# The projection products of two embedding stages, issued in four lots inside the feed-forward stage ahead of each

## The reference, cut to what matters

```python
    for layer in range(DEPTH):
        j = layer // 2
        hn = rmsnorm(h, g_mix[layer])
        if layer % 2 == 0:
            mix = even_mixer(hn, ...)
        else:
            mix = odd_mixer(hn, positions, ...)
        h = h + mix
        h = h + swiglu(rmsnorm(h, g_ffn[layer]), w_gate[layer], w_up[layer], w_down[layer])
        gate = jax.nn.sigmoid(rmsnorm(h, g_ple[layer]) @ w_ple_gate[layer])
        h = h + gate * (p[layer] @ w_ple_proj[layer])
```

## Time and profile before

| | |
|---|---|
| median of 3 runs | 1310.94 us |
| lowest and highest | 1304.89 and 1313.02 us |
| span of the profiled execution | 1305.6 us |
| device time of the profiled execution | not given by the page |
| TensorE busy | 1226.4 us, 94% |
| VectorE, ScalarE busy | 727.1 and 462.5 us |

### The profile page before, as it was taken

One profiled execution on the slowest core, in us unless ns is written; L12 is line 12 of the kernel. 1 busy time (PEld: TensorE's weight loads), 2 busy tenths in 40 slices (PEclk: granted clock), 3 DMA queues, 4 the chain that ended last, 5 costly groups with the idle time before them and its releaser, 6 DMA issues.

```text
span 1305.6 us, 16407 instructions
## 1 busy us (share of the span) xinstructions
PE 1226.4 (94%) x6372; PEld 839.8 (64%) x6372; DVE 727.1 (56%) x1358; ACT 462.5 (35%) x741; POOL 28.8 (2%) x61
## 2 busy tenths in 40 slices
PE   6998999999898989999988997899999999999995
PEld 5997888876676768888866965544444444454442
DVE  5787877785657768777868997511221222221212
ACT  5444444444555654444454425211111111111112
POOL 0000000000000000000000300000000000000000
PEclk9999999999998999999999998899999999999999
DMA  8467777753430196666533464989999999999994
GB/s 286 158 224 268 255 258 257 257 194 117 166 129 1 65 364 249 247 246 245 200 138 129 146 200 149 407 324 413 421 430 430 428 428 428 429 429 429 428 429 168
DMA packets 120060, 358.09 MB, mean 274 GB/s; under 512 B 8666, under 2 KB 67731, under 8 KB 104626
## 3 DMA queue, kind: packets, MB, share of 16 engines
q1 hardware_dynamic: 113408, 331.85, 65.5%
q0 software_dynamic: 6336, 25.17, 4.9%
q10 hardware_dynamic: 242, 0.06, 0.0%
HBM read 352.58 MB, written 1.05 MB: 271 GB/s over the span
## 4 chain that ended last, share of the span: by engine, by line
PE 80%; DVE 12%; ACT 3%; DMA 2%; issue 1%; ACTq 0%; SPq 0%; DVEq 0%
PE ps L2702 16%; PE ps L419 14%; PE ps L420 14%; PE ps L421 14%; PE ps L2733 8%; PE ps L2691 4%; DVE xn L2302 3%; DMA second_expert<-in_moe_w_up 2%; DVE w_lo L393 2%; PE ps L2747 1%; PE ps L1023 1%; PE ps L2748 1%; PE ps L894 1%; PE ps L1635 1%; PE ps L829 1%
## 5 line engine op out<-in xcount | busy, mean ns | idle before, releaser
L393 DVE TENSOR_TENSOR w_lo<-dense_weights,w_hi 128x1024 fp32r<-128x1024 f32 (+1 forms) x228 | 273.1, 1211 | 100.9 <-ACT w_hi L388 100.2
L388 ACT CAST w_hi<-dense_weights 128x1024 fp32r<-128x1024 f32 (+1 forms) x228 | 234.9, 1042 | 257.7 <-PE ps L421 225.6
L419 PE MATMUL ps<-w_hi,xT_lo 128*128 128x512 f32 (+1 forms) x608 | 244.9, 403 | 19.1 <-DVE xT_lo L2349 5.2
L420 PE MATMUL ps<-w_lo,xT_hi 128*128 128x512 f32 (+1 forms) x608 | 238.4, 392 | 0.0
L421 PE MATMUL ps<-w_hi,xT_hi 128*128 128x512 f32 (+1 forms) x608 | 237.9, 391 | 0.0
L419 PEld LDWEIGHTS ps<-w_hi,xT_lo 128*128 128x128 f32 x608 | 116.2, 191 | 48.0 <-issue 14.9
L421 PEld LDWEIGHTS ps<-w_hi,xT_hi 128*128 128x128 f32 x608 | 116.2, 191 | 24.6
L420 PEld LDWEIGHTS ps<-w_lo,xT_hi 128*128 128x128 f32 x608 | 116.4, 191 | 23.3 <-issue 0.7
L2840 DVE TENSOR_TENSOR hnT<-ps,g_bc 128x512 f32<-128x512 f32 x32 | 22.1, 692 | 157.3 <-PE ps L2733 157.3
L2849 DVE SCALAR_TENSOR_TENSOR cmask<-g_v,ps 128x256 f32<-128x256 f32 x32 | 13.5, 421 | 166.5 <-ACT g_v L2791 166.5
L2791 ACT ACTIVATE g_v<-ps 128x256 f32<-128x256 f32 x32 | 12.3, 384 | 206.0 <-PE ps L2702 206.0
(11 more groups left out here) (407 smaller groups left out, 1725.1 us busy)
## 6 DMA issues: line engine op xcount, KB each, us to landing
ada_w<-in_ada_w POOLq DMA_DIRECT2D x12, 2048.0 KB, 11.7
dense_weights<-in_w_gate SPq DMA_DIRECT2D x22, 1024.0 KB, 7.2
dense_weights<-in_w_up SPq DMA_DIRECT2D x22, 1024.0 KB, 9.4
dense_weights<-in_w_down SPq DMA_DIRECT2D x22, 1024.0 KB, 5.0
dense_weights<-in_moe_w_gate SPq DMA_DIRECT2D x11, 2048.0 KB, 19.0
dense_weights<-in_moe_w_up SPq DMA_DIRECT2D x11, 2048.0 KB, 23.4
second_expert<-in_moe_w_gate SPq DMA_DIRECT2D x11, 2048.0 KB, 18.4
second_expert<-in_moe_w_up SPq DMA_DIRECT2D x11, 2048.0 KB, 22.9
```

What stands on the lines that cost most here:

```text
L388: act.copy(split_view(w_hi, name, i, j), piece(name, i, j)).then_inc(hi_ready, 1)
L393: dve.tensor_tensor(split_view(w_lo, name, i, j), piece(name, i, j), split_view(w_hi, name, i, j).bitcast(F32), ALU.subtract).then_inc(pie ...
L419: pe.matmul(out, left[1], right[0], start=start, stop=False)
L420: pe.matmul(out, left[0], right[1], start=False, stop=False)
```

## The change

Both projections get a place of their own in g_bc and are loaded by one transfer each: the first behind the loads of ev_in, the second behind those of od_out, once the query products have been made. The eight matmuls of a layer are cut into four lots of two, (i, t) for column half i and token tile t, each with a bank 2i + t that keeps it until VectorE reads it in the embedding stage:

- (1,1), bank 3: behind the gate and up product of the first feed-forward block;
- (0,0), bank 0: behind the transposes of the last hidden block, ahead of its down product;
- (0,1), bank 1: behind the last down product;
- (1,0), bank 2: one matmul behind the norm's second bank of transposes, one behind the fourth.

The norm's transposes ahead of the embedding go to banks 4, 6, 5, 7 in place of 0 to 3, and the gate products to banks 4, 6 and 5, 7. In layer 1 `pe_sums` moves to the middle of the first gate product, VectorE's `dve_cols` ahead of the first additions to h, and TensorE waits for these columns before the second gate product. The final gain's semaphore is shared with the projections' transfers.

```diff
-ITEMS = [... ("ple0", 2, 1, 1), ... ("ple1", 2, 1, 1), ...]
+ITEMS = [... ("ple0", 2, 1, 0), ... ("ple1", 2, 1, 0), ...]
...
+        ple_proj = g_bc
...
@@ ups
                 load_b("od_up", 1, q_up_rows[2], q[:, 2])
+                sp.wait_ge(ple_used, 1)
                 for k in range(2):
                     sp.dma_start(q_up_rows[k], q[:, k]).then_inc(small_landed, 16)
...
+            def projection(layer):
+                if layer == 1:
+                    sp.wait_ge(odd_up.lat_turned, 2)
+                sp.dma_start(ple_proj[:], a["w_ple_proj"][layer].rearrange("(k p) n -> p k n", p=P)).then_inc(ple_landed, 16)
...
             columns("ev_in", a["ev_w_in"][0], [2048, 1536, 512, 1024, 0])
+            projection(0)
...
             columns("od_out", a["od_w_out"][0], [0, 512])
+            projection(1)
             ffn(1)
...
@@ NormStage
-                return ps[:, c // 2 + (4 if self.index == 0 else 0), (c % 2) * S:(c % 2 + 1) * S]
+                banks = {0: (4, 5, 6, 7), 2: (4, 6, 5, 7), 5: (4, 6, 5, 7)}.get(self.index, (0, 1, 2, 3))
+                return ps[:, banks[c // 2], (c % 2) * S:(c % 2 + 1) * S]
...
                     last.then_inc(self.turned, 1)
+                    if between is not None and b in between:
+                        between[b]()
...
@@ FfnStage.pe
                     if n >= 1:
                         down(n - 1, it)
+                    else:
+                        projection.up(pe, 1, 1)
+
+                projection = ple[self.layer]
                 self.run(pe, step)
                 turn(last_block, None)
+                projection.up(pe, 0, 0)
                 down(last_block, None)
+                projection.up(pe, 0, 1)
...
@@ PleStage
+            GATE_BANKS = ((4, 6), (5, 7))
+
+            def up(self, pe, i, t, ks=range(2)):
+                if (i, t) == (1, 1):
+                    pe.wait_ge(ple_landed, 16 * (self.layer + 1))
+                for k in ks:
+                    last = pe.matmul(ps[:, 2 * i + t, :], pT[:, self.layer, k, t * P:(t + 1) * P],
+                                     ple_proj[:, k, i * 512:(i + 1) * 512], start=(k == 0), stop=(k == 1))
+                if (i, t, k) == (1, 0, 1):
+                    last.then_inc(ple_used, 1)
...
-                tokens_by_columns(pe, self.name, 0, (0, 1), rest=lambda: self.norm.wait_rest(pe))
-                up(0)
+                def rest():
+                    self.norm.wait_rest(pe)
+                    if self.between is not None:
+                        self.between.pe_sums(pe)
+
+                tokens_by_columns(pe, self.name, 0, self.GATE_BANKS[0], rest=rest)
                 if self.between is not None:
-                    self.between.pe_sums(pe)
-                tokens_by_columns(pe, self.name, 1, (4, 5), rest=lambda: up(1))
+                    pe.wait_ge(self.between.cols, 1)
+                tokens_by_columns(pe, self.name, 1, self.GATE_BANKS[1])
                 if self.following is not None:
-                    stay_busy(pe, 3, 6)
+                    stay_busy(pe, 4, 6)
...
@@ PleStage.dve
                     if i == 1 and self.between is not None:
-                        self.between.dve_cols(dve, own)
                         split_upto(dve, split_lo, self.name, i, 2)
                         conformer.spread_weights(dve, own, 0, 4)
                     split_upto(dve, split_lo, self.name, i, 3)
-                    dve.wait_ge(ple_used, 2 * self.layer + i + 1)
+                    if i == 0 and self.between is not None:
+                        self.between.dve_cols(dve, own)
+                    dve.wait_ge(ple_used, self.layer + 1)
...
-            norms[2].pe(pe)
+            norms[2].pe(pe, between={1: lambda: ple[0].up(pe, 1, 0, (0,)), 3: lambda: ple[0].up(pe, 1, 0, (1,))})
...
-            norms[5].pe(pe)
+            norms[5].pe(pe, between={1: lambda: ple[1].up(pe, 1, 0, (0,)), 3: lambda: ple[1].up(pe, 1, 0, (1,))})
```

More of the change, by code:

```diff
@@ L57 @@
 SLOTS = 2
-ITEMS = [("ev_in", 5, 1, 0), ("ev_out", 2, 2, 0), ("ffn0", FF_BLOCKS, 2, 1), ("ple0", 2, 1, 1), ("od_in", 5, 2, 0),
-         ("od_up", 2, 0, 1), ("od_out", 2, 1, 0), ("ffn1", FF_BLOCKS, 2, 1), ("ple1", 2, 1, 1), ("conv_in", 4, 2, 0),
+ITEMS = [("ev_in", 5, 1, 0), ("ev_out", 2, 2, 0), ("ffn0", FF_BLOCKS, 2, 1), ("ple0", 2, 1, 0), ("od_in", 5, 2, 0),
+         ("od_up", 2, 0, 1), ("od_out", 2, 1, 0), ("ffn1", FF_BLOCKS, 2, 1), ("ple1", 2, 1, 0), ("conv_in", 4, 2, 0),
          ("conv_out", 2, 1, 0)]
@@ L326, in build @@
         pieces_used = sem("pieces_used")
-        ple_used = sem("ple_proj_used")
+        ple_landed, ple_used = sem("ple_proj_then_gain_landed"), sem("ple_proj_used")
         up_used = sem("od_up_used")
@@ L522, in load_b @@
                     sp.wait_ge(up_used, 4)
-                elif stage is not None and stage.startswith("ple"):
-                    sp.wait_ge(ple_used, 2 * int(stage[-1]) + k + 1)
                 elif stage is not None:
@@ L568, in ple @@
                 w = a["w_ple_gate"][layer].rearrange("(k p) n -> p k n", p=P)
-                q = a["w_ple_proj"][layer].rearrange("(k p) n -> p k n", p=P)
                 for i in range(2):
                     load_a(name, i, [cols8(part_a(name, i))], [w[:, :, i * 512:(i + 1) * 512]])
-                    load_b(name, i, part_b(name, i)[:, 0:2 * 512].rearrange("p (k n) -> p k n", k=2),
-                           q[:, :, i * 512:(i + 1) * 512])
+            def projection(layer):
+                if layer == 1:
+                    sp.wait_ge(odd_up.lat_turned, 2)
+                sp.dma_start(ple_proj[:], a["w_ple_proj"][layer].rearrange("(k p) n -> p k n", p=P)).then_inc(ple_landed, 16)
             columns("ev_in", a["ev_w_in"][0], [2048, 1536, 512, 1024, 0])
+            projection(0)
             w = a["ev_w_out"][0].rearrange("(k p) n -> p k n", p=P)
@@ L816, in factors, with pe @@
                 dve.tensor_tensor(rstd[:, 2], rstd[:, 0], rstd[:, 1], ALU.mult).then_inc(self.made, 1)
-            def pe(self, pe, gains=None):
+            def pe(self, pe, gains=None, between=None):
                 if gains is not None:
@@ L1013, in __init__ @@
                 self.layer, self.name, self.norm, self.between, self.following = layer, f"ple{layer}", norm, between, following
-            def pe(self, pe):
[L1016 to L1025, removed]
-                tokens_by_columns(pe, self.name, 0, (0, 1), rest=lambda: self.norm.wait_rest(pe))
-                up(0)
+            GATE_BANKS = ((4, 6), (5, 7))
[7 more added lines that the diff above has]
+                    last.then_inc(ple_used, 1)
+            def pe(self, pe):
+                def rest():
[3 more added lines that the diff above has]
+                tokens_by_columns(pe, self.name, 0, self.GATE_BANKS[0], rest=rest)
                 if self.between is not None:
-                    self.between.pe_sums(pe)
-                tokens_by_columns(pe, self.name, 1, (4, 5), rest=lambda: up(1))
+                    pe.wait_ge(self.between.cols, 1)
+                tokens_by_columns(pe, self.name, 1, self.GATE_BANKS[1])
                 if self.following is not None:
-                    stay_busy(pe, 3, 6)
+                    stay_busy(pe, 4, 6)
             def act(self, act):
@@ L1045, in act @@
                             act.wait_ge(self.used, 2 * (2 * self.layer + i - 1) + t + 1)
-                        act.activation(ple_th[:, t], ps[:, 4 * i + t, :], ACT.Tanh,
+                        act.activation(ple_th[:, t], ps[:, self.GATE_BANKS[i][t], :], ACT.Tanh,
                                        scale=rstd[:, 1, t:t + 1]).then_inc(self.tanh, 1)
@@ L1061, in dve @@
                         dve.wait_ge(self.tanh, n)
-                        dve.scalar_tensor_tensor(out=ple_a[:, t], in0=ple_th[:, t], scalar=1.0, in1=ps[:, 4 * i + 2 + t, :],
+                        dve.scalar_tensor_tensor(out=ple_a[:, t], in0=ple_th[:, t], scalar=1.0, in1=ps[:, 2 * i + t, :],
                                                  op0=ALU.add, op1=ALU.mult).then_inc(self.used, 1)
@@ L2893, in __init__ @@
                 self.made = [sem(f"fin_made{t}") for t in range(T)]
-                self.f_landed = sem("fin_gain_landed")
+                self.f_landed = ple_landed
             def load(self, sp):
@@ L2909, in dve @@
             def dve(self, dve, own):
-                dve.wait_ge(self.f_landed, 16)
+                dve.wait_ge(self.f_landed, 48)
                 for half in range(2):
```

## The result

The changed kernel takes 1293.21 us (median of 6 runs, 1290.76 to 1299.49), the kernel before 1309.35 (6 runs). The ratio is 0.9886, 95% interval 0.9866 to 0.9906: 14.9 us less, and the profiled execution's span went from 1305.6 to 1289.6. Two more measurements of the same kernel, made with the experiments, gave 0.9907 and 0.9901. So the change makes the kernel faster by 12 to 15 us (10 to 17.5 by the ends of the intervals), where 9.1 were forecast and 13.7 were called the most that it can give.

A forecast was written before the change was run, and what follows sets the result against it. TensorE, busy 94% of the span, was taken as the bound: 6.0 us from the first embedding stage plus 3.1 from the second give 9.1 off 1310.9, so 1301.8 us, range 1296 to 1309.

The forecast's parts named there:

- the turn on VectorE: End of the second embedding stage: VectorE's work replaces the removed work, so of the last 3.43 us only 1.28 arrive.
- the prediction's own signs of being wrong: VectorE idle before the last additions to h, a projection load waited for, or the clock staying low in the convolution's stage.
- The unit and what is removed: Gate products: a split product's pass takes 0.227 us; removing four groups of four takes 13.7 us off TensorE, 6.86 per stage.
- Lot (1,1): First feed-forward block: the lot of 1.72 us fits in TensorE's 2.26 us wait for ff_hid, usable 2.42; cost 0.
- Lots (0,0) and (0,1): Around the last down product: waits of 1.95 and 1.38 us take them; cost 0, and transposes beginning 0.18 later.
- Lot (1,0), 0.82 with the one before: Halves among the norm's transposes, 16 taken as 2.24 us without a stop: gate product 0.82 us later per layer.
- The columns: Second embedding stage: TensorE waits for VectorE's modulation columns before the second gate product; cost 0.4 us with pipeline refilling.
- VectorE's spreads: End of the second embedding stage: weight spreads and splits make VectorE 2.15 us late for the additions to h.
- The longer pause: Before the transposes behind the second embedding stage: idle time grows from 1.98 to about 4.1 us, lowering the clock; cost 0.4.
- B: Rival: VectorE isn't late, spreads or clock cost nothing, both embedding stages gain in full, 11.7 us: 1299.2 us. Chance 0.26.
- C: Rival: lots 3 and 4, (0,1) and (1,0), push the gate product by their whole 3.43 us: 1307.0 us. Chance 0.16.
- D: Rival: the longer pause keeps the convolution's input product at 1.2 GHz, so the kernel is slower: 1313.9 us. Chance 0.03.

The follow-up runs named there:

- fill2: The kernel before with two filler matmuls of 128x512 (1.7 us) behind the first block's gate and up product, nothing else changed: ratio 0.9986 to the kernel before.
- fill1: The kernel before with one filler matmul of 0.86 us in the first feed-forward step's wait: 1302.33 us in a single run, beside 1308.9 for the kernel before.
- late11: The changed kernel with lot (1,1) moved behind lot (0,1), ahead of the transposes: 1301.98 us, ratio 0.9941 to the kernel before.
- spreads: The changed kernel with two of VectorE's four weight spreads taken out of the stretch ahead of the last additions to h: 1294.03 us, against 1296.55 on the same chip.
- best: The changed kernel with the weight spreads taken apart and VectorE's modulation columns one split earlier: 1293.38 us, against 1296.01 for the changed kernel on the same chip.
- again: The changed kernel with nothing edited, run once more for a second profile: ratio 0.9907 to the kernel before.

## Why the prediction was wrong

The direction, the place and the turn on VectorE were right; the time was outside the range, at 1293.2 against 1296.0. By how much it lies outside is partly chance, as the same kernel had medians of 1296.55 and 1296.01 in the other two comparisons. That the gain is 14.3 us and not 9.1 isn't. A gain over 1% had been given a chance of 0.19 and came, with 1.1%. None of the prediction's own signs of being wrong appeared: VectorE had no idle time ahead of the additions, no load was waited for, and the clock was low in one short stretch ahead of the convolution's product (692.8 to 696.2 us in the first profile), not throughout its stage. Step by step:

- **The unit and what is removed**: right. 6.89 us went in the first embedding stage, and 6.86 were forecast for the removed products.
- **Lot (1,1), "cost 0"**: this is the step that failed. It looked at the wait of 2.26 us and whether the lot fits in, and not at the passes behind it. The row of 118.96 stood among the rows with no clock beside it, and only the pause of the first layer's tail was looked at for its clock. From 120.12 to 123.10 us eight passes in a row start 0.42 to 0.43 us apart instead of 0.227. The lot costs nothing and brings 1.56 and 1.59 us: 3.1 us that were missing, and with them falls the sentence that 13.7 is the most the change can give, on which the lower end of the range was built. fill2 and fill1 show the gain without the rest of the change, and late11 shows half of it lost again.
- **Lots (0,0) and (0,1)**: 0 and 0.18 forecast; the wait of 0.23 left over and 0.14 later transposes were measured.
- **Lot (1,0), 0.82 with the one before**: too dear. Eight transposes take 0.87 us (656.79 to 657.66), so 16 take 1.74 and not 2.24: in the kernel before, the merged row of 2.29 us hid a stop for the last of the four additions to h, done at 668.94, behind which the ninth transpose starts at 669.00. The first half of the lot now fills it. All four lots together cost 0.14 a layer instead of 0.82: 1.4 us of gain more than forecast for both layers.
- **The columns**: 0.4 forecast, about 0.35 measured (33.43 us in spreads against 33.07 in best).
- **VectorE's spreads**: 2.15 forecast, 2.0 measured, and given back in full when they are taken apart.
- **The longer pause**: the pause of 4 us came as said, and the clock fell behind it in three of three profiles of the changed kernel, between 692 and 701 us (a stretch of the first profile, and one of again):

```profile
692.00:697.00 5.00, 4.33 (x22) 3.76 (x22) 3.53 (x7) 5.00 (x11) 0.00 (x0) 0.66 0.24 58
697.00:702.00 5.00, 4.48 (x22) 3.91 (x22) 3.37 (x6) 4.87 (x11) 0.00 (x0) 0.66 0.23 69
```

  It cost 0.03, 0.25 and 0.08 us and not 0.4, counted from the first transpose to the steady passes of the product behind it (8.93 us in the kernel before, 8.96, 9.18 and 9.01 in these three), as TensorE waits for xT_lo there. The Trainium skill's rule ("TensorE: Matmul & The Clock Gate", "What's actually happening") holds for the clock itself: the page says that the default is throttled and that activity releases it, and here the clock fell behind all three pauses of 4 us and behind 5 of 6 unfilled waits of 2.3 us. But the 1.7 us that the prediction drew from it for the long pause were at most 0.25, and at the first feed-forward step, where the same rule spoke for the change, the prediction didn't apply it.

With the measured sizes the sum is 13.7 + 3.1 - 0.3 - 0.35 - 2.0 = 14.2 us, against 14.3 in the stage times, and 14.9, 12.2 and 13.0 us in the three comparisons. The profiles differ in the low stretches in the odd mixer and the experts, by up to 4.5 us in a stage; no more can be said of the difference between the comparisons.

Of the rivals, B (VectorE isn't late) was nearest in time at 1299.2 and wrong in cause; C was refuted by the lots' 0.14 us; D did not happen, the clock was low in that one stretch, which cost 0.25 us at most.

## What to carry to other kernels

When work is moved into a wait, look at the pace of the passes behind the wait and at the granted clock there, not only at whether it fits in: filling a wait can bring nearly as much again as the work that is moved, here 1.6 us beside a lot of 1.7. When an engine is relieved ahead of a join, work out when the other engine would arrive, and move what stands in its way in the same change. A slowed stretch costs only where the slowed engine is the last to arrive; ahead of a wait for another engine it is free, and a filler that would prevent it gains nothing.

## What the runs showed of the hardware

- One matmul of 0.86 us in a wait of 2.3 us kept TensorE at the higher of its two levels in both layers (fill1, one profile); two did so in the 16 cases of eight profiles. Without them it fell to the lower one in 5 of 6 cases, for a loss of 1.56 to 1.6 us each.
- Over all twelve profiles the granted clock fell within 2 us of the end of each of the five pauses of 4 us, of each of the twelve waits of 2.1 us in the odd mixer (ending at 399.9 us in the kernel before), of 8 of the 10 unfilled waits of 2.74 in the first layer's tail, of 3 of the 4 waits of 2.4 behind it, of one of the 7 waits of 1.98 and of one of the 8 of 1.95. The length of the wait alone doesn't decide it.
- Behind equal waits (2.26 us, in late11) the clock fell once and not the other time, and between three profiles of one kernel the stretch from the first layer's tail through the odd mixer took 139.9 to 144.6 us with the low stretches in other places. So a single profile's stage time can be off by some 4 us where such waits stand; the other stages agreed to 0.04 us in the profiles compared here, but for the 1.6 us that fill2 lost in one.
